# Products of query columns over 258 columns instead of 260, in a hybrid decoder layer on one core

## The reference

```
xn = rmsnorm(h);  proj = xn @ w_in                       # 2048 x 15384
A: forgetting attention of 8 heads;  ya = oa @ w_a_o
B: yb = (sc_b * dwconv3(sc_c * sc_h)) @ w_b_o
C: gated linear attention of 4 heads;  yc = (silu(rc) * rmsnorm(oc)) @ w_c_o
h = h + (sum_i sigmoid(gate_i(xn)) * y_i) @ w_o          # w_o 2048 x 2048
u = dwconv3(rmsnorm(h) @ w_up)                           # w_up 2048 x 11264
h = h + (silu(u_gate) * u_up) @ w_down                   # w_down 5632 x 2048
return rmsnorm(h)[:, 16:]
```

## Time and profile before

| | |
|---|---|
| median of 3 runs | 1738.51 us (1738.46 to 1738.52) |
| profiled execution, own time | 1738.35 us |
| its span, first to last instruction | 1736.5 us |
| around the span | 1.85 us |
| PE busy, weight loads busy | 1725.9 us (99%), 1674.7 us (96%) |
| DVE, ACT, POOL busy | 1117.6 us (64%), 763.9 us (44%), 263.5 us (15%) |
| share of the last chain on PE, on L1438 | 98%, 81% |
| granted TensorE clock | 0.999 of full speed |

### The profile page before, as it was taken

One profiled execution on the slowest core, in us unless ns is written; L12 is line 12 of the kernel. 1 busy time (PEld: TensorE's weight loads), 2 busy tenths in 40 slices (PEclk: granted clock), 3 DMA queues, 4 the chain that ended last, 5 costly groups with the idle time before them and its releaser, 6 DMA issues.

```text
span 1736.5 us, 34095 instructions
## 1 busy us (share of the span) xinstructions
PE 1725.9 (99%) x13429; PEld 1674.7 (96%) x13429; DVE 1117.6 (64%) x1607; ACT 763.9 (44%) x921; POOL 263.5 (15%) x494
## 2 busy tenths in 40 slices
PE   9999999999999999999999999999999999999998
PEld 8999999999999999999999999999999999888886
DVE  6857766667565555555556687777777777644554
ACT  6635454354354443444444444334444434343443
POOL 4153332630530000000000033421000000000000
PEclk9999999999999999999999999999999999999999
DMA  8667657666566665566655566666555655656664
GB/s 234 170 180 187 169 149 199 176 177 177 153 188 182 184 177 184 171 192 193 195 168 191 184 192 197 205 200 189 184 181 181 189 183 175 229 192 191 191 194 134
DMA packets 310299, 320.67 MB, mean 185 GB/s; under 512 B 17353, under 2 KB 285133, under 8 KB 310093
## 3 DMA queue, kind: packets, MB, share of 16 engines
q1 hardware_dynamic: 296861, 311.01, 59.6%
q0 software_dynamic: 12928, 7.80, 2.0%
q10 hardware_dynamic: 432, 0.79, 0.1%
HBM read 311.10 MB, written 2.11 MB: 180 GB/s over the span
## 4 chain that ended last, share of the span: by engine, by line
PE 98%; DVE 1%; DMA 0%; ACT 0%; issue 0%; SPq 0%; ACTq 0%; DVEq 0%
PE ps L1438 81%; PE ps L1717 5%; PE ps L1715 5%; PE ps L1716 5%; PE ps L1545 1%; DVE xl L942 0%; PE ps L1559 0%; DMA xa<-in_meta_tokens_dram 0%; PE ps L1584 0%; PE ps L1574 0%; DVE lo L897 0%; PE ps L1575 0%; PE ps L1603 0%; PE ps L1604 0%; PE ps L1531 0%; PE ps L1520 0%
## 5 line engine op out<-in xcount | busy, mean ns | idle before, releaser
L897 DVE TENSOR_TENSOR lo<-raw,hi 128x1024 fp32r<-128x1024 f32 x584 | 710.0, 1229 | 485.0 <-ACT hi L628 482.7
L628 ACT CAST hi<-raw 128x1024 fp32r<-128x1024 f32 x584 | 605.3, 1049 | 663.6 <-PE ps L1438 535.5
L1438 PE MATMUL ps<-xh,hi 128*128 128x260 f32 (+1 forms) x3312 | 532.9, 283 | 0.2 <-DVE xl L942 0.2
L1438 PE MATMUL ps<-xl,hi 128*128 128x260 f32 (+1 forms) x3312 | 530.0, 282 | 0.0
L1438 PE MATMUL ps<-xh,lo 128*128 128x260 f32 (+1 forms) x3312 | 529.6, 282 | 0.0
L1438 PEld LDWEIGHTS ps<-xh,hi 128*128 128x128 f32 x3312 | 452.4, 188 | 1.4 <-issue 0.4
L1438 PEld LDWEIGHTS ps<-xl,hi 128*128 128x128 f32 x3312 | 452.2, 188 | 0.0
L1438 PEld LDWEIGHTS ps<-xh,lo 128*128 128x128 f32 x3312 | 452.1, 188 | 0.0
L611 POOL DMA_DIRECT2D hT<-h2b x128 | 69.3, 550 | 602.1 <-DVE h2b L1290 597.3
L1717 PE MATMUL ps<-lo,act_h 128*128 128x512 f32 x350 | 137.3, 392 | 0.0
L1716 PE MATMUL ps<-hi,act_l 128*128 128x512 f32 x350 | 136.8, 391 | 0.0
(11 more groups left out here) (304 smaller groups left out, 1251.4 us busy)
## 6 DMA issues: line engine op xcount, KB each, us to landing
raw<-in_w_in_dram SPq DMA_DIRECT2D x224, 512.0 KB, 3.8
raw<-in_w_up_dram SPq DMA_DIRECT2D x176, 512.0 KB, 4.6
raw<-in_w_down_dram SPq DMA_DIRECT2D x88, 512.0 KB, 4.7
raw<-in_w_o_dram SPq DMA_DIRECT2D x32, 512.0 KB, 3.7
raw<-in_w_in_dram SPq DMA_DIRECT2D x32, 256.0 KB, 4.1
raw<-in_w_a_o_dram SPq DMA_DIRECT2D x16, 512.0 KB, 4.5
raw<-in_w_b_o_dram SPq DMA_DIRECT2D x16, 512.0 KB, 3.8
raw<-in_w_c_o_dram SPq DMA_DIRECT2D x16, 512.0 KB, 3.4
```

Of the source, the lines that this page charges most:

```text
L628: nc.scalar.copy(part(ph, i, q, hi_all), raw[:, s, :]).then_inc(hi_ready, 1)
L897: nc.vector.tensor_tensor(part(ph, i, q, lo_all), raw[:, s, :], part(ph, i, q, hi_all).bitcast(F32), ALU.subtract).then_inc(lo_ready, 1)
L1438: ins = nc.tensor.matmul(pset(st, n)[:, m, a:], tiles(weights, s, j, m), moving(j)[side][:, a:], start=first and (kind, at) == (0, 0), sto ...
```

## The change

The panels whose result is needed at 258 positions are multiplied over 258 columns from `Q0` instead of 260 from `C0`. That is `sc_b`, the attention's queries and the swish gate in the branch stage, all of `GT`, all of `WO` and all of `UP`. The sums go to the columns from `QW` on, so that DVE finds them where it found them before. The two columns ahead are no longer written or read. A moving row now begins at byte 56 of its 1088 instead of byte 48, and ends where it ended. All else stays.

```diff
@@ use_turns
                             a = 0 if m else skip
-                            ins = nc.tensor.matmul(pset(st, n)[:, m, a:], tiles(weights, s, j, m), moving(j)[side][:, a:],
+                            acc = pset(st, NC)[:, m, QW:] if n == NQ else pset(st, n)[:, m, a:]
+                            ins = nc.tensor.matmul(acc, tiles(weights, s, j, m), moving(j)[side][:, a:],
                                                    start=first and (kind, at) == (0, 0), stop=last and (kind, at) == (2, KJ - 1))
@@ branch stage
-            window = [(C0, NC)] * 3 + [(0, T)] * 4 + [(C0, NC)] * 2
+            window = [(C0, NC)] * 2 + [(Q0, NQ)] + [(0, T)] * 4 + [(Q0, NQ)] * 2
@@ gate_trip
-                        mv = x_window(kq * KJ, C0, NC)
+                        mv = x_window(kq * KJ, Q0, NQ)
...
-                        mv = (lambda g, k0: lambda j: (bo_h[:, g, k0 + j, C0:T], bo_l[:, g, k0 + j, C0:T]))(g, kq * KJ)
+                        mv = (lambda g, k0: lambda j: (bo_h[:, g, k0 + j, Q0:T], bo_l[:, g, k0 + j, Q0:T]))(g, kq * KJ)
...
-                    use_turns(GT, i, q, st, mv, NC, kq == 0, kq == last, turned(q // 4 + 1) if q < 12 and not settled else ROWS)
+                    use_turns(GT, i, q, st, mv, NQ, kq == 0, kq == last, turned(q // 4 + 1) if q < 12 and not settled else ROWS)
@@ output projection
-                    use_turns(WO, i, q, st, (lambda k0: lambda j: (mix_h[:, k0 + j, C0:T], mix_l[:, k0 + j, C0:T]))(kq * KJ),
-                              NC, kq == 0, kq == 3)
+                    use_turns(WO, i, q, st, (lambda k0: lambda j: (mix_h[:, k0 + j, Q0:T], mix_l[:, k0 + j, Q0:T]))(kq * KJ),
+                              NQ, kq == 0, kq == 3)
@@ up_trip
-                    use_turns(UP, i, q, st, x_window(kq * KJ, C0, NC), NC, kq == 0, kq == 3)
+                    use_turns(UP, i, q, st, x_window(kq * KJ, Q0, NQ), NQ, kq == 0, kq == 3)
```

## The result

The changed kernel takes 1745.22 us (median of 6 runs, 1745.02 to 1747.06). The kernel before takes 1738.41 us on the same chip (6 runs, 1738.13 to 1738.52). The ratio is 1.0041, 95% interval 1.0028 to 1.0054: 6.8 us or 0.4% slower. The forecast was slower by 11.2 us, in the range from 1729 to 1761.

A forecast was written before the change was run, and what follows sets the result against it. The prediction took PE as the bound, by number of matmuls times their distance. A start's +2.0 ns less 0.83 ns for two columns, times 9600, gave +11.2 us: 1749.6 us, range 1729 to 1761.

The forecast's parts named there:

- What bounds the kernel: Whole kernel: PE, busy 1725.9 of 1736.5 us, is never fed late; time is number of matmuls times their distance.
- The sum: Over 9600 shortened matmuls: +2.0 - 0.83 = +1.17 ns each, +11.2 us; chance 0.35 for 1742 to 1754 us.
- The two columns: In each shortened matmul, two columns less at 2.4 GHz save 0.83 ns, -8.0 us in all.
- the shifted start: In each shortened matmul, a row beginning 8 past a multiple of 16 bytes costs 2 ns; ends 0 and 3.
- the 2 ns of L1603: Two-pass float32 matmuls of 258 columns of `pt0`: second head's shifted start averages 382 against 380 ns, taken as price.
- the 10 ns of each distance that the columns don't explain: Up projection: 118.33 ns a matmul against 108.3 for 260 columns; the start's price might hide in the rest.
- The columns count, the start doesn't: Rival for the shortened matmuls: the 8 bytes are free, -8.0 us, 1730.4 us; faster had chance 0.29.
- No less work, no change: Rival for the shortened matmuls: fetch or weight load sets the pace, 118.3 ns and 1738.4 us stay; chance 0.16.
- The lines of 16 bytes: Row fetch in 16-byte pieces: 260 and 258 columns both touch 65, so the change is worth 0.
- A floor: Weight load as pace of the matmuls: last twelve, of 256 columns, take 119 ns each, no less than 260 columns.
- The full price of 3 ns: Rival for the shortened matmuls: each shifted start stalls 3 ns, +20.8 us, 1759.2 us; chance 0.2.
- The down panels' 4.7 ns: Down projection: rows beginning 16 bytes earlier took 228.6 instead of 233.3 ns; bounds the shift at 4.7 ns either way.

The follow-up runs named there:

- the first experiment: Changed kernel with its 258 columns begun at the old start, byte 48, against the kernel before: 1769.12 us, ratio 1.0177.
- the starts: Kernel before, up projection's trips 1 to 21 in seven stretches of 258 columns from different start columns: one run, 1745.59 us.
- the third experiment: Kernel before, 260 columns everywhere, activation tiles 8 bytes later: 1786.58 us, ratio 1.0277; 122.22 ns in the up projection, 123.33 in the gates.

## Why the prediction was right in its number, and where its step failed

*What bounds the kernel* was right: the time is the number of matmuls times their distance, no wait explains the difference of the medians, rows of 272 columns and the down projection stayed, and what the shorter matmuls lost reached the end undiminished. 6.9 us of distances account for 6.8 us of the median.

*The sum* was right in sign and near in size: +1.17 ns and 11.2 us forecast, +0.84 ns in the up projection, +0.72 ns over all 9600 and 6.8 us measured. In it both terms were wrong. The two columns, priced at -0.83 ns, measured +3.3 ns at the old start and -3.1 to -4.2 at the new one (119.17 against 122.22 and 123.33); the shifted start, priced at +2 ns, measured +3.9 to +5 ns with 260 columns and -2.5 ns with 258. The failed step is the one that took the 2 ns of L1603 for a price of the start and added a price of the columns to it. The row was thinner than it looked: the 383 ns belong to a pass that follows a 128-column matmul of L1605, the 380 ns beside it to one that follows L1438. The second passes, each behind a first pass of L1603, last 381 and 380 ns. The step's own condition, "unless it hides in the 10 ns of each distance that the columns don't explain", was the place to stop at: those 10 ns are the cost that moves. That +2 - 0.83 came close to +0.84 is luck and no evidence for either term.

*The rivals.* "The columns count, the start doesn't" needed 117.4 ns and has fallen with the change itself and with the first experiment. "No less work, no change" named two mechanisms. The lines of 16 bytes have fallen, as above. A floor does show, at 111.67 ns, and the weight load may set it, but it lies some 7 ns below, where it decides nothing alone. The full price of 3 ns has fallen with the starts: the ones it speaks of are the cheaper ones with 258 columns. The down panels' 4.7 ns, which the prediction kept as an end of the range "of either sign", were the nearest relative of what happened.

*What is shown* is what the distance depends on: the row's start, its length, the succession of the rows, and the place of the weights' tiles, with a period of 256 bytes in the two pairs tried. Each combination holds one distance over hundreds of matmuls, between 115.8 and 125.0 ns for 248 to 268 columns; the third experiment's two distances are the one exception. *What isn't shown* is the mechanism inside the chip. That the fetches of a moving row and of the next weights meet in the memory, more or less often according to both places, is argued only, and by what rule it would go the runs don't say. Open too are the two distances of one and the same setting in the third experiment, why many combinations end at exactly 118.33 ns, and what part of the first experiment's 3.3 ns the accumulator's column 2 has.

The Trainium skill, on the page "TensorE: Matmul & The Clock Gate" (section Back-to-back issue gap), says that in a stream of weight loads and matmuls both set the spacing. The runs agree in kind: shorter rows end at a floor that the columns don't explain. The formula that the prediction took from that section, N / 2.4 + 2.5 ns, is given there for a matmul alone and not for such a stream. The estimate by it for 258 columns is 110.0 ns; here they lay between 118.3 and 122.0, depending on where things lie, which the formula doesn't know.

## What to carry to other kernels

Where PE is the bound and a chain's distance is several nanoseconds above its columns, price nothing in the start or the length of a row by itself: the next neighbour may be dearer with less work in it. Split one stage of the kernel into stretches with different starts, lengths, orders or weight places, and read length by matmuls in the chain: seven settings come out of one run, and the two that were also run as whole kernels gave the same distance there. Two halves of a change that each measure several nanoseconds don't have to sum to what both do.

## What was not expected of the hardware

- 192 and 224 columns both take 111.67 ns with a weight load each: a floor for these matmuls, though not for all: the four of 16 columns in the earlier trace rows stand at 103 ns.
- Distances lock: 258 columns at 119.17 in the up projection and the gates alike, although DVE, ACT and DMA do other work beside them.
- In the two pairs tried, the weights' place acts with a period of 256 bytes (-256 as 0 in the up projection, -272 as -16 in the down projection); the worst place tried cost 2.8 ns of 119 on 258 columns and 4.8 ns of 229 on 512.
